# Selected key blocks of the sample branch fetched one by one, two samples to an attention item

## The reference, cut to what matters

```python
def nsa_cmp_sel(q, kv_cmp, kv_sel, q_pos, pe, w1, w2):
    ...
    p = masked_softmax(s, cmask)                       # compressed branch
    imp = jnp.einsum('bgrtn,nj->bgtj', p, overlap)
    ...
        forced = (jsel[None, :] == 0) | ((dist >= 0) & (dist < N_LOCAL))
        rank = jnp.where(valid, impi + BIG * forced.astype(jnp.float32), -BIG)
        _, idx = lax.top_k(rank, k_top)
        kvg = ks[bi, gi, idx].reshape(B, N_KV_B, qb, k_top * SEL_BLOCK, 2, HD_B)
        ...
        sc = jnp.einsum('btgrd,bgtkd->bgrtk', qi, kvg[..., 0, :]) * ATT_SCALE
        pr = masked_softmax(sc, kmask[:, :, None])
        return jnp.einsum('bgrtk,bgtkd->btgrd', pr, kvg[..., 1, :])
```

## Time and profile before

| | us |
|---|---|
| median of 3 runs | 2640.61 (2637.81 to 2641.68) |
| the profiled execution | 2638.68 |
| its span, first to last instruction | 2636.3 |
| PE busy | 2572.9 (98%) |
| DVE / ACT / GpSimd busy | 1501.9 / 939.1 / 1458.4 |
| granted TensorE clock, mean | 0.994 |

### The profile page before, as it was taken

The page is one execution under the profiler, slowest core; times in us unless marked ns, Lnnn a source line. Parts: engine busy times, 40 slices in busy tenths (PEclk is TensorE's granted clock), DMA queues, the critical chain, the costliest instruction groups (busy, mean ns, idle before and its releaser), DMA issues.

```text
span 2636.3 us, 51872 instructions
## 1 busy us (share of the span) xinstructions
PE 2572.9 (98%) x21479; PEld 2478.3 (94%) x21479; DVE 1501.9 (57%) x1952; ACT 939.1 (36%) x1631; POOL 1458.4 (55%) x948
## 2 busy tenths in 40 slices
PE   8999989999999999999999999999999999999998
PEld 8999978987787899999999999999999999999998
DVE  6112375877665227555576678345346554677676
ACT  4100034656667224333333333210134333333332
POOL 6332200112323367877798885543559777788881
PEclk9999999999999999999999999999999999999999
DMA  6112453351204623354464431311323434563431
GB/s 202 41 34 65 121 147 101 97 178 49 95 21 138 248 80 138 114 175 145 179 221 165 154 129 49 129 57 40 105 105 113 153 135 155 190 245 137 139 127 65
DMA packets 199266, 328.26 MB, mean 125 GB/s; under 512 B 11277, under 2 KB 126738, under 8 KB 195386
## 3 DMA queue, kind: packets, MB, share of 16 engines
q1 hardware_dynamic: 189712, 306.02, 34.3%
q0 software_dynamic: 2880, 10.49, 1.1%
q10 hardware_dynamic: 6442, 8.46, 1.0%
HBM read 233.22 MB, written 95.90 MB: 125 GB/s over the span
## 4 chain that ended last, share of the span: by engine, by line
PE 89%; DVE 5%; issue 2%; POOL 2%; ACT 1%; DMA 1%; SPq 0%; ACTq 0%; DVEq 0%; POOLq 0%
PE psum L957 21%; PE psum L933 21%; PE psum L484 16%; PE psum L532 7%; PE psum L976 3%; PE psum L2347 2%; PE psum L2814 2%; PE psum L2844 2%; PE psum L2340 1%; PE psum L520 1%; PE psum L2320 1%; PE psum L3713 1%; PE psum L2783 1%; PE psum L3396 1%; PE psum L562 1%
## 5 line engine op out<-in xcount | busy, mean ns | idle before, releaser
L957 PE MATMUL psum<-part_hi,whl 128*128 128x258 f32 x3136 | 507.8, 284 | 1.2 <-POOL whl L397 1.0
L957 PEld LDWEIGHTS psum<-part_hi,whl 128*128 128x128 f32 x3136 | 434.2, 189 | 1.9 <-POOL whl L397 1.4
L484 PE MATMUL psum<-xhi,whl 128*128 128x344 f32 x1776 | 329.2, 320 | 2.1 <-DVE qT L1676 1.0
L1240 DVE TENSOR_TENSOR xlo_plain<-xlo_plain,psum 128x516 f32<-128x516 f32 x360 | 245.2, 688 | 141.7 <-PE psum L957 139.3
L933 PE MATMUL psum<-shi,whl 128*128 128x258 f32 x1920 | 323.9, 283 | 0.0
L454 POOL TENSOR_TENSOR whl<-wraw,zeroc 128x1024 fp32r<-128x1024 f32 x62 | 120.4, 1942 | 357.4 <-PE psum L484 171.8
L957 PE MATMUL psum<-part_lo,whl 128*128 128x258 f32 x1568 | 315.0, 282 | 0.0
L484 PEld LDWEIGHTS psum<-xhi,whl 128*128 128x128 f32 x1776 | 288.2, 188 | 2.6 <-issue 2.6
L933 PEld LDWEIGHTS psum<-shi,whl 128*128 128x128 f32 x1920 | 271.5, 190 | 0.0
L933 PE MATMUL psum<-xhi,whl 128*128 128x258 f32 x1440 | 249.6, 285 | 4.1 <-POOL whl L365 4.1
L957 PEld LDWEIGHTS psum<-part_lo,whl 128*128 128x128 f32 x1568 | 243.2, 190 | 0.0
(11 more groups left out here) (532 smaller groups left out, 5249.3 us busy)
## 6 DMA issues: line engine op xcount, KB each, us to landing
part_raw<-b_spill SPq DMA_DIRECT2D x98, 516.0 KB
b_spill<-rows_H SPq DMA_DIRECT2D x78, 516.0 KB, 3.9
rows<-in_cache_cmp_kv SPq DMA_DIRECT2D x128, 128.0 KB, 2.6
raw_even<-in_w_ffn SPq DMA_DIRECT2D x16, 1024.0 KB, 5.9
out_even<-in_w_ffn SPq DMA_DIRECT2D x16, 1024.0 KB, 6.2
out_odd<-in_w_ffn SPq DMA_DIRECT2D x16, 1024.0 KB, 6.0
raw_odd<-in_w_ffn SPq DMA_DIRECT2D x14, 1024.0 KB, 6.9
wraw<-in_w_in_ab SPq DMA_DIRECT2D x26, 512.0 KB, 4.4
```

The source lines that it names most:

```text
L484: last = pe.matmul(psum[:, 3 * bset + c, 0:TC], w, rhs[ah][:, k0 + k, c * TC:(c + 1) * TC], start=(k == 0 and n == 0), stop=(k == kn - 1 a ...
L957: last = pe.matmul(psum[:, 2 * p + h, 0:QT], out_weights(first, n, wh)[:, k, p % 2, :], (part_hi, part_lo)[ah][x][:, k, h * QT:(h + 1) * Q ...
L1240: event(dve.tensor_tensor(quarters(out_total(i, p)), quarters(out_total(i, p)), two_banks(p), ALU.add))
```

## The change

The selected branch no longer reads all rows of a sample. `dve_block_choice` now makes a list `chosen` of 13 block numbers (physical ones, with the page table folded in) for each row of a sample and head. For each sample and each key/value group, an engine loads one number at a time into a register and issues a transfer of that block's half (16 partitions, 8 pieces of 256 bytes each). The forced blocks come by two further transfers a sample (`forced_rows`). So a sample's rows fill two tiles of 128 partitions instead of four, two samples make one item, and `ITEMS` goes from ten to six. The mask addition on DVE goes; two small matmuls of -1e30 (`negs`) after the scores take its place for one block, and maximum and exponential read PSUM directly. SP issues the blocks of samples 0 to 3, 5 and 6 and one group of sample 4; GpSimd issues the other group of sample 4, one block behind each of its weightings in tiles 6 and 7, and sample 7 behind them. The indirect gathers go. The small sample steps move from tiles 4 to 7 to tiles 2 to 5.

```diff
-        SAMPLE_STEPS = ((4, 5), (4, 9), (5, 4), (5, 8), (6, 6), (7, 7))
+        SAMPLE_STEPS = ((2, 3), (2, 7), (3, 5), (3, 8), (4, 5), (5, 3))
...
                     if heads_of(i) == 1:
                         head_weights("s", i, h)
+                        if i >= 6:
+                            chosen_block(pool, 4, 1, h // 2 + (0, 8)[i - 6], s_s4)
...
-        ITEMS = ("w0", "s0", "s1", "s2", "s3", "s4", "w1", "s5", "s6", "s7")
+        ITEMS = ("s0", "s1", "w0", "w1", "s2", "s3")
+        DYNAMIC = 13
...
+        def chosen_block(eng, b, g, x, sem_):
+            r = HB * b + 4 * g
+            i, k = (0, x + 1) if x < 7 else (1, x - 7)
+            block = eng.value_load(chosen[r:r + 1, x:x + 1])
+            eng.dma_start(srows[b // 2][2 * (b % 2) + i][16 * k:16 * k + 16, :]
+                          .rearrange("p (x g d) -> p x g d", g=2, d=64)[:, :, g, :],
+                          blocks_of_table[bass.ds(block, 1), :, :, g, :].rearrange("n m x d -> (n m) x d"))\
+                .then_inc(sem_, 16)
...
+            sp.wait_ge(sD, DVE_S["chosen"])
+            for b in range(5):
+                chosen_rows(sp, b, (0,) if b == 4 else (0, 1))
             sp.wait_ge(p_ql, 2 * NT)
             sp.wait_ge(p_qk, soft_no[job_no[("c", NT - 1, 0)]] + 1)
...
+            forced_rows(sp, 5)
+            sp.wait_ge(p_qk, soft_no[job_no[("s", NT - 1, HB - 1)]] + 1)
+            window_rows(1)
+            chosen_rows(sp, 5, (0, 1))
+            new_rows(1)
+            sp.wait_ge(p_qk, len(SOFT))
             window_rows(2)
             window_rows(3)
+            forced_rows(sp, 6)
+            chosen_rows(sp, 6, (0, 1))
             new_rows(2)
             new_rows(3)
-            sp.wait_ge(sP, PE_S[f"V{place('s3')}"])
+            sp.wait_ge(sP, PE_S[f"V{place('s1')}"])
...
-            gather(pool, cache_sel[0], srows[BUFFER[1]], 1, rows_sem(1))
...
+            chosen_block(pool, 4, 1, 12, s_s4)
+            forced_rows(pool, 7)
+            chosen_rows(pool, 7, (0, 1))
```

More of the change, by code:

```diff
@@ L3152, in build @@
         ACT_S = steps("cmp", *act_selected(), "rowexp", "hi")
-        DVE_S = steps("gg", "pgz", "masks", "qe", "cmpmax", "pcs", "pgsel", "cmpw", "knz", "pre",
+        DVE_S = steps("gg", "pgz", "masks", "qe", "cmpmax", "pcs", "chosen", "cmpw", "knz", "pre",
                       *dve_selected(), "rowd", "osel1", "wrow", "wsel", "pnT", "osb", "lo")
@@ L3358, in pe_gate_spread @@
                 for i in range(4):
-                    pe.matmul(psum[32 * i:32 * i + 32, 3, 8 * half:8 * half + 8], ident[0:R, c],
-                              selneg[:, 8 * i:8 * i + 8], start=True, stop=True)
-                for i in range(4):
                     pe.matmul(psum[32 * i:32 * i + 32, 3, 16 + half:17 + half], ident[0:R, c], g64[:, 2:3],
@@ L3387, in pe_keys_back @@
                 pe.wait_ge(s_wr[b // 2], 32)
-                source = [wrow[(b // 2) % 2][:, b % 2, e, 0:P] for e in range(4)]
+                source = [wrow[b // 2][:, b % 2, e, 0:P] for e in range(4)]
             if p and i >= 2:
@@ L3405, in scores @@
                 if p >= 2:
-                    if selected(p - 2):
-                        pe.wait_ge(sD, DVE_S[f"ma{p - 2}"])
-                    else:
-                        pe.wait_ge(sA, ACT_S[f"ex{p - 2}"])
-                n = number(p)
-                half = n // 4 if selected(p) else n
+                    pe.wait_ge(sA, ACT_S[f"ex{p - 2}"])
                 for i in range(4):
-                    b = n if selected(p) else 4 * half + i
+                    b = sample_of(p, i)
+                    half = b // 4
                     last = pe.matmul(psum[32 * i:32 * i + 32, p % 2, :], qm[:, b, 32 * half:32 * half + 32],
-                                     keys_tile(p)[:, i, :], start=True, stop=True)
+                                     keys_tile(p)[:, i, :], start=True, stop=not selected(p), skip_group_check=True)
+                if selected(p):
+                    for i in (1, 3):
+                        last = pe.matmul(psum[32 * i:32 * i + 32, p % 2, :].rearrange("p (e k x) -> p e k x", e=4, k=8)[:, :, 6, :],
+                                         identb[:, 32 * i:32 * i + 32], negs[:, :, :], start=False, stop=True,
+                                         skip_group_check=True)
                 done(last)
@@ L3527, in act_key_copy @@
             if i == 0 and p >= 2:
[L3528 removed]
+                act.wait_ge(sP, PE_S[f"S{p - 2}"])
             act.activation(keys_tile(p)[:, i, :], psum[:, key_bank(p, i), :], ACT.Copy).then_inc(sA, 1)
```

288 lines of the change are left out of this document (139 added, 149 removed).

## The result

The changed kernel takes 2677.26 us in the median of 4 runs (2675.82 to 2678.02), the kernel before 2641.14 us beside it. The ratio is 1.0137 (95% interval 1.012 to 1.0155): 36 us slower. The profiled execution took 2677.39 us, its span is 2675.8 us, its mean granted clock 0.983.

What follows compares the result with a forecast made beforehand. PE bounds the kernel, but SP's block issue was to delay it: first output product +8.2 us (897.6 against 889.4), clock drop +1.7, so +9.9 on the profiled execution; difference put on the median 2640.6: 2650.5 us, range 2634 to 2676.

Steps and rivals of the forecast that it cites:

- The gain: Sample items on PE: four fewer at 4.49 us each save 18.0 us; the added mask matmuls cost 0.5 us.
- d: SP's issue time for one chosen block, load plus transfer: 0.95 us taken, from 0.80 to 1.15.
- T: SP's time for one transfer: 0.52 us with 32 partitions, 0.67 with 64.
- L: SP's time for one register load: 0.30 to 0.50 us, after the assertion and perhaps the address arithmetic go.
- Chain (a): SP's list from DVE's choice to w1's new row, issued at 710.4 + 169 d; shift 169 d - 150.7 us.
- (b): SP's list behind tile 7's last selected scores: new row issued at 820.5 + 52 d; shift 52 d - 40.6 us.
- The choice: DVE's list of chosen blocks, ready for SP at 704 us; 4 us of push estimated, bounds nothing and 8.
- From t to the output: From t, w1's first keys on PE (873 us), to the first output product: 24.6 us, including 19.9 from reload to split unit.
- The clock: Granted clock drops for a stretch after a PE wait; one drop likely, +1.7 us.
- Prompt attention: New DVE time exposed there: 3 us later, bounds 0 and 5, already counted in (b).
- very late: Rival: d above 1.05, by loads waiting for their results or GpSimd's last 29 above 2.3 us; +27 to +60, chance 0.17.
- SP keeps up: Rival: cheaper 16-partition transfers let 52 blocks behind tile 7 take under 34 us; -5 to -11.5 us, chance 0.15.

Runs made afterwards that it cites:

- the run without loads: Changed kernel with SP's blocks of samples 0 to 3, 5 and 6 from fixed places, one piece a partition, no register load: 2636.5 us (0.998).
- the last version: Changed kernel with sample 4, eleven sample 3 blocks and part of sample 6 on GpSimd, sample 5's blocks filling SP's standstill, late reload: 2636.5 us (0.9982).
- the steps alone: Kernel before with only the six sample steps moved from tiles 4 to 7 to tiles 2 to 5: 2638.7 us (0.9991).

## Why the prediction was wrong

The mechanism and the place were right: SP's queue issues without a pause from 707 us, PE stands still ahead of w1's keys behind one new row, the reload follows, GpSimd is idle until the unit lands. The size was off, 36 us in place of 10, and the step that failed is the price of one block. Step by step, on the profiled execution:

- **The gain.** Right. The scores of the last items start at 906.73 and 911.22 us, 4.49 apart, as before; with SP cheap the gain shows in the time (2636.5).
- **The price of a block, d: the term that failed, and in it T, the transfer.** I took 0.95 us, in the middle of 0.80 to 1.15. It is 1.08: (125.67 + 28.60 + 26.94) / 169 = 1.07, and a load ahead of each of the three groups. Split as in the prediction, the load L is right at its low end: from the start of a load to the address arithmetic behind it are 0.30 us in the median, so the 147 ns arithmetic and the assertion of the earlier trace rows did fall away. T, from there to the next load, is 0.75 us in the median and 0.78 in the mean, with single transfers of up to 1.56. I had it at 0.52 to 0.67, from rows with 32 partitions in one piece each and with 64 partitions. The same stretch was 0.50 us in the kernel before, with an instruction of 0.316; the new shape's takes 0.564, and it is the two pieces or more a partition that cost the 0.25 us. No row had this shape, and both of my bounds stood below it. At 1.69 us for each 0.01 us of d the error of 0.13 us became 22 us. The formula itself holds: with d = 1.08 it gives 169 x 1.08 - 150.7 = +31.8, that is 2672 us.
- **Chain (a) decides, not (b).** I had them equal. SP came to the wait for tile 7 at 835.4, 14 us behind the last selected maximum (821.29 us). Thirteen blocks less ahead of it gave 13 us.
- **The choice** at 704 us: it came at 707.0, within the bounds of 8, and as (a) decides, those 3 us count in full. In the fifteen profiles of the changed kernel and of the versions with SP's loads for samples 0 to 3 it came between 700.3 and 713.1, 706.6 in the mean.
- **From t to the output,** 24.6 us: measured 27.3 (898.54 to 925.81). The reload's 19.9 are exact; the stretch of PE in front of it took 7.3 in place of 4.7, at half clock (its key products 1.97 us in place of 1.09).
- **The clock.** I took 1.7 us for one drop. It is 2.6 us in that stretch, and 3.1 us more are lost behind the first output product, where the clock of 0.92 over 34 us is worth 2.7. That the waits of 11 and 28 us cause these 3.1 isn't shown. In the run without loads and in the last version, with waits for rows of 2.6 and 0.8 us, the 34 us behind the product have a clock of 0.93; there as here PE had just waited over 5 us for the weight unit. In the kernel before, without such a wait, they have 1.00.
- **Sum:** 3.0 for the choice, 22.0 for d, 0.6 for the other transfers, 2.6 for the clock: 28.2, the distance from 897.6 to 925.81. With the rest of the clock, 1.4, and 0.8 less around the span that is 28.8 of profiled time, from 2648.6 to 2677.4.
- **Prompt attention,** 3 us, bounds 0 and 5. The last selected maximum stands 8.1 us later than in the earlier trace rows. In the sixteen profiles of the changed kernel and its versions it stands between 814.5 and 827.3 us, 820.4 in the mean, so only 1 us of the 8 is this execution's. The kernel before has one profile, of an execution 2.5 us under its median. One piece of it is seen to be the change's: from 622 to 636 us PE is busy 10.9 to 11.3 of 14 us in all sixteen, against 13.57 before and 12.82 with the steps alone. There PE has a wait of some 2.6 us for a weighting on DVE, which stands behind the small operations of the masks (625.2 to 629.5 us in the changed kernel). The whole of what the change adds there isn't settled; that the moved steps cost nothing is (2638.7).
- **GpSimd's blocks.** Right that they are hidden, wrong in price: 0.94 us apart when back to back, not 1.6. Sample 7 was out at 851 us, not 862, and GpSimd then did nothing for 70 us. That is the room in which every better version stands.

Of the rivals, "very late" came, at d = 1.08, but not by the way that I gave it. "SP keeps up" had the issue of a 16-partition transfer cheaper than any shape seen; it is dearer than both of the earlier trace rows (0.564 us against 0.316 and 0.469). A register load used at once takes 0.264 to 0.288 us, and loading ahead saved 0.05 us a block in one run and none in another.

The Trainium skill, page "DMA: Bandwidth & Descriptors", section "Latency and other measured facts", has a floor of about 600 ns for a tensor_load; the 208 loads here are under half of it in the median, and do not agree.

The forecast's "SP keeps up" put 11.5 us of gain at d = 0.6. The run without loads, at 0.5, had 4.5: t was 856.0, not 853.3, the part from t to the output 26.1 us, and from the output product to the end it took 4.7 us longer than the kernel before.

## What to carry to other kernels

When a bulk transfer is cut into many small ones, count them, and price one by the whole of its issue: load, address arithmetic, transfer and the gaps between them, taken as the period of a run of them. A range from the nearest rows is no bound when the new shape differs in a way that none of them has: the guess at what would fall away from the load was right here, and the pieces of a partition, which no row had, were not covered. With 169 in a row an error of 0.1 us is 17 us, so such a forecast needs a range as wide as that product. Then ask what stands behind them in the same queue: here a 2 KB transfer and the reload that the next stage needs; and look for the engine that sits idle at that time before giving all to one queue.

## What the runs showed of the hardware

- SP's instruction for a 32 KB transfer of 16 partitions takes 0.316 us with one piece a partition and 0.562 to 0.564 us with 2, 4 or 8.
- From a fixed address the eight-piece form took 0.598 us (median), no less than the 0.564 by register; what falls away is the load and the address arithmetic.
- GpSimd issued the same transfer in 0.53 us and a block with its load every 0.94 us, SP every 1.05 to 1.10.
- Blocks of 32 KB land 2.2 us after their issue, but 7.0 (GpSimd's) and 7.7 us (SP's) in the median while 4.1 MB of reload are under way. Of SP's, those issued just behind the reload took 10 to 13 us and landed with its end.
